# A fourth seven-product pair in each MLP layer, and an earlier release of the ring slots of summed blocks

## The chip, the cores and the metric

The kernel runs on one core of a Trainium2 chip. Its time is the device time of one execution in microseconds (us); less is better. The engines are named as in the profile: PE (matrix products), DVE (vector), ACT (scalar), POOL (the general one, which here issues small transfers) and SP (which issues the loads of the weights). They run at the same time, each through its own program in order, and wait for one another through semaphores.

## What is computed

A network of three blocks on 256 tokens of width 2048, all in float32. The change lies in the MLP of the first two blocks (depth 2, width 8192):

```python
def squared_relu_mlp(h, w1, w2):
    z = jax.nn.relu(h @ w1)
    return (z * z) @ w2
# h: 256 x 2048, w1: 2048 x 8192, w2: 8192 x 2048; once in each of two layers
x = x + squared_relu_mlp(rms_norm(x, ffn_norm[i]), w_ff1[i], w_ff2[i])
```

Before and behind the MLPs stand projections, attention, a recurrent unit and a third block, which the change leaves as they are.

## The kernel before

**Slabs.** Every weight is read once from DRAM in slabs of 256 rows by 512 columns (512 KB). A product of the 256 x 2048 activations with 512 columns of a weight is a group (`g14`, `g15`, ...) of eight slabs. A slab goes through four steps: SP loads it into one of four slots of the ring `raw`; ACT rounds it into `whi`; DVE subtracts and writes the rest into `wlo`; PE multiplies. `whi` and `wlo` have four slots too, so ACT can't begin slab n before PE is done with slab n-4 (`act.wait_ge(mm, n + 1 - RAW)`). The precision of float32 is kept by three products (activation high by `whi`, high by `wlo`, low by `whi`), for two rows of 128 in the slab and two halves of 128 tokens: 12 matmuls of 128x512.

**Seven products for eight.** For some pairs of groups of `w_ff1` the 2 x 2 blocks (two halves of the tokens, two halves of the 2048 rows, two groups of 512 columns) are multiplied in Winograd's form of Strassen's scheme: seven products instead of eight, with sums of blocks as factors. Such a pair has seven stages `p1`, `p2`, `p5`, `p3`, `p6`, `p7`, `p4` of four half slabs each. A half slab is a slab that is multiplied with one half of the tokens only: 6 matmuls. The pair is 28 half slabs (168 matmuls) in place of 16 slabs (192 matmuls), and each half slab is rounded and split like a slab. The sums are built in four buffers `chain_raw` (`qk`, `prob` and two halves of `mkv`): `p1` is loaded straight into them; for `p5`, `p6` and `p4` DVE adds a raw block to them (`chain_sum`), and ACT and DVE then split the sum, not the raw block; for `p7` DVE writes a difference into the raw slot (`u3`). DVE does these sums two tasks ahead: behind the split of task n stands the sum for task n+2. A pair loads 24 slabs (`p6` loads none, it sums the block of `p3` once more).

**The order.** `plan()` writes it out by hand. A slab has a number v, eight to a group; `number_all` puts a half slab behind the slab v at which `pair_of` has set it (28 half slabs spread evenly from `first` to `last`), and numbers all tasks n. Other work stands in lists for each engine under a v and runs when the engine has done its part of slab v: so `epi_add`, with which DVE adds a finished group of `w_ff2` from PSUM (`acc[g % 2]`) to x, and the parts of a pair's end (`part_n2`, `part_n1`, `relu_...`, `part_square`, `turned`: 16 small transfers issued by POOL, then `tail`). Group g uses the same half of PSUM as group g-2, so PE begins it only when the `epi_...` of group g-2 is done:

```python
if begins:
    if of >= 2:
        pe.wait_ge(out_of[of % 2], of // 2)
```

**The layers.** An MLP is cut into four chunks of 2048 columns of `w_ff1`, each followed by the four groups of `w_ff2` that use it. `PAIRS` says for each chunk how many of its two pairs of groups take the seven products. The half slabs of a chunk are woven into the slabs of the chunk ahead of it, since they depend on nothing of it. Below, f is the number v of the first `w_ff2` slab of the chunk they are woven into; in layer 0 the third chunk has f = 208. A layer takes 3 pairs in the kernel before, 2 layers 6 pairs.

Of the kernel before, what the change touches and what calls it, by code (L numbers as in the profile page):

```python
# [308 lines left out]
FF2_EVEN = ((0, 1), (2, 3), (4, 5), (6, 7))  # L309


PAIRS = (0, 1, 1, 1)


STAGES = (("p1",), ("p2",), ("p5",), ("p3", "p6"), ("p7",), ("p4",))
CHAIN = {"p1": 0, "p5": 1, "p6": 2, "p4": 3}
BLOCKS = {"p1": (0, 0), "p2": (1, 0), "p5": (0, 1), "p3": (1, 1), "p6": (1, 1), "p7": (0, 0), "p4": (1, 0)}
SUMS = {"p5": 0, "p7": 1, "p3": 2, "p6": 3}
QUARTERS = NK // 2 // SLAB_K


def plan():
# [92 lines left out]
    def ffn(layer, rst, a, z, next_rst, next_gain):  # L415

        waiting = []
        for c, count in enumerate(PAIRS):
            gs = [sc.group(f"w_ff1{layer}", 0, D * c + GW * i, a) for i in range(2 * count, 4)]
# [25 lines left out]
            for n, left in at_need:  # L445
                sc.groups[fs[n // S]].need[n % S] = [("tail_lo", sc.tails - left)]
            more = PAIRS[c + 1] if c < NCHUNK - 1 else 0
            if more == 1:
# [180 lines left out]
def build(nc, A, out):  # L629
# [6 lines left out]
    with ctx:  # L636
# [7 lines left out]
        def sem(name):  # L644
            return ctx.enter_context(nc.semaphore(name))
# [161 lines left out]
        sm = {n: sem(n) for n in names}  # L807
# [17 lines left out]
        def raw_of(task):  # L825
            return raw[:, task.raw * SLAB:(task.raw + 1) * SLAB]
# [5 lines left out]
        def tokens(t, lo, n, width):  # L832

            return t[:, 0:TB * width].rearrange("p (b n) -> p b n", b=TB)[:, :, lo:lo + n]
# [38 lines left out]
        def block_of(part, stage):  # L873

            k, n = BLOCKS[stage]
            pair = sc.pairs[part.pair]
            row, col = P * (k * NK // 2 + SLAB_K * part.j), D * pair.chunk + pair.col + GW * (1 - n)
            return W[f"w_ff1{pair.layer}"][row:row + SLAB_K * P, col:col + GW].rearrange("(t p) n -> p t n", p=P)

        def chained(part, stage):  # L880

            if stage == "p1":
                return sm[f"chain_in{part.j}"], 16 * (part.pair + 1)
            return sm["chain_add"], QUARTERS * (3 * part.pair + CHAIN[stage] - 1) + part.j + 1

        def in_rows(t):
            return t.rearrange("p (t n) -> p t n", t=SLAB_K)
# [41 lines left out]
        @block.sync  # L929
        def _(sp):  # L930
            def slot_free(task):

                last = task.before
                if last is None:
                    return
                if last.part and last.part.stage == "p3":
                    sp.wait_ge(sm["chain_add"], QUARTERS * (3 * last.part.pair + CHAIN["p6"] - 1) + last.part.j + 1)
                sp.wait_ge(w_lo, last.n + 1)

            def slab(task):  # L940
                of, k, _, _ = sc.slab_of(task.g, task.s)
                of = sc.groups[of]
                slot_free(task)
                dst = raw_of(task)
                row = of.row + k * SLAB_K * P
                src = W[of.w][row:row + SLAB_K * P, :]
                if of.pieces:
                    src = src[:, 0:2 * QKW].rearrange("(t p) (m c) -> p t m c", p=P, m=2)
                    dst = dst.rearrange("p (t m c) -> p t m c", t=SLAB_K, m=2)
                    for k in range(SLAB_K):  # L950
                        sp.dma_start(dst[:, k], src[:, k, :, of.col:of.col + GW // 2])\
                            .then_inc(ld[task.raw], 16)
                else:
                    sp.dma_start(in_rows(dst), src[:, of.col:of.col + GW].rearrange("(t p) n -> p t n", p=P))\
                        .then_inc(ld[task.raw], 16)

            def part_load(task):
                part = task.part
                if part.stage == "p6":
                    return  # L960
                if part.stage == "p1":
                    pair = sc.pairs[part.pair]
                    if pair.first:
                        sp.wait_ge(sm["sum_lo"], 4 * (pair.layer + 1))
                    else:
                        sp.wait_ge(w_lo, sc.pairs[part.pair - 1].parts["p4", part.j].n + 1)
                    sp.dma_start(in_rows(chain_raw[part.j]), block_of(part, "p1"))\
                        .then_inc(sm[f"chain_in{part.j}"], 16)
                    return
                slot_free(task)  # L970
                sp.dma_start(in_rows(raw_of(task)), block_of(part, part.stage))\
                    .then_inc(ld[task.raw], 16)

            def memory(i):

                sp.dma_start(tokens(mem, GW * i, GW, D),
                             A["mem"][0].rearrange("(b p) n -> p b n", p=P)[:, :, GW * i:GW * (i + 1)])\
                    .then_inc(sm[f"mem{i}_in"], 16)

            for task in sc.stream:  # L980
                if task.part:
                    part_load(task)
                    continue
                if task.n < D // GW:
                    memory(task.n)
                slab(task)

            o = out[0].rearrange("(b p) n -> p b n", p=P)
            for i, (b, c, n) in enumerate(FINAL):
                sp.wait_ge(sm["fin_ok"], i + 1)  # L990
                sp.dma_start(o[:, b, c:c + n], y[:, D * b + c:D * b + c + n]).then_inc(sm["out_done"], 16)
            sp.wait_ge(sm["out_done"], 16 * len(FINAL))
# [125 lines left out]
        def _(act):  # L1118
# [9 lines left out]
            def hi(task, fold=None):  # L1128
                part, n = task.part, task.n
                c = slice(task.slot * SLAB, (task.slot + 1) * SLAB)  # L1130
                if part and part.stage in CHAIN:
                    act.wait_ge(*chained(part, part.stage))
                    src = chain_raw[part.j]
                else:
                    src = raw_of(task)
                    if part and part.stage == "p7":
                        act.wait_ge(sm["u3_ok"], QUARTERS * part.pair + part.j + 1)
                    else:
                        act.wait_ge(ld[task.raw], 16 * task.loads)
                if n >= RAW:  # L1140
                    act.wait_ge(mm, n + 1 - RAW)
                if fold is None:
                    A_(whi[:, c], src, ACT.Copy).then_inc(w_hi, 1)  # L1143
                    return
                for (t, c), (_, r) in zip(rows_of(task.slot), rows_of(task.raw)):
                    ins = A_(whi[:, c], raw[:, r], ACT.Copy, scale=gain_of(fold, SLAB_K * task.s + t))  # L1146
                ins.then_inc(w_hi, 1)
# [347 lines left out]
        def _(dve):  # L1495
# [22 lines left out]
            def u3(task):  # L1518

                dve.wait_ge(ld[task.raw], 16 * task.loads)  # L1520
                dve.wait_ge(*chained(task.part, "p6"))
                V.tensor_tensor(raw_of(task), chain_raw[task.part.j], raw_of(task), ALU.subtract).then_inc(sm["u3_ok"], 1)

            def chain_sum(task):

                part = task.part
                if part.stage == "p6":
                    task = sc.stream[sc.pairs[part.pair].parts["p3", part.j].n]
                t = chain_raw[part.j]
                dve.wait_ge(ld[task.raw], 16 * task.loads)  # L1530
                dve.wait_ge(*(chained(part, "p1")))
                V.tensor_tensor(t, t, raw_of(task), ALU.add).then_inc(sm["chain_add"], 1)  # L1532
# [941 lines left out]
```

## Time and profile before

| | us |
|---|---|
| median of 3 runs (2952.87 to 2954.57) | 2954.24 |
| the profiled execution's own time | 2953.56 |
| its span, first to last instruction | 2951.8 |
| PE busy | 2914.2 |
| DVE busy | 2054.6 |
| ACT busy | 1619.7 |

The span is what the trace shows; 1.8 us of the profiled execution's own time lie around it. Matmuls overlap in their records (each is shown with 390 ns, the next starts 227 ns later), so a busy PE is not a measure of its speed; what counts is whether PE waits, and the distance from one matmul's start to the next. The sums of the pairs (L1532) run from 370.3 to 807.6 us in the first MLP, and the last one of the second starts at 1892.9 us.

### The profile page before, as it was taken

The numbers are of one execution on the slowest core, as the hardware profiler recorded it, in microseconds if no ns is written. First come the engines' busy times: TensorE is split into PE (matmuls) and PEld (weight loads), VectorE is DVE, ScalarE is ACT, GpSimd is POOL, SyncE is SP. The second block draws the span as 40 slices with busy tenths as digits, with TensorE's granted clock in tenths as the row PEclk, the third lists the DMA queues.
The fourth block names the chain that finished last, engine by engine and source line by source line (L and its number), as shares of the span: only waits on it lengthen the run. The fifth ranks groups of instructions, "written<-read, shape, count | busy, mean of one in ns | idle before, by whom it ended". The sixth has DMA issues, their size and how long they took to land.

```text
span 2951.8 us, 35199 instructions
## 1 busy us (share of the span) xinstructions
PE 2914.2 (99%) x12996; PEld 2399.3 (81%) x12996; DVE 2054.6 (70%) x2679; ACT 1619.7 (55%) x2134; POOL 634.6 (21%) x1257
## 2 busy tenths in 40 slices
PE   8999999999999999999999999999999999999998
PEld 7888888888888778788888888888888887878887
DVE  6537777777766777877786777856557777887555
ACT  6445555555554566755655555545444456775433
POOL 0003312212033310013212122123324663100210
PEclk9999999999999999999999999999999999999999
DMA  7446777776677655556767777766776776666774
GB/s 264 165 151 202 237 231 248 230 253 221 227 228 234 206 171 161 166 167 213 242 222 247 228 248 236 233 215 217 236 216 199 220 227 187 209 205 207 249 255 157
DMA packets 351628, 636.94 MB, mean 216 GB/s; under 512 B 38240, under 2 KB 63200, under 8 KB 350688
## 3 DMA queue, kind: packets, MB, share of 16 engines
q1 hardware_dynamic: 306448, 566.30, 60.6%
q0 software_dynamic: 44432, 67.45, 7.2%
q8 instruction: 102, 1.67, 0.2%
q10 hardware_dynamic: 576, 0.94, 0.1%
q14 instruction: 70, 0.57, 0.1%
HBM read 586.31 MB, written 10.49 MB: 202 GB/s over the span
## 4 chain that ended last, share of the span: by engine, by line
PE 85%; DVE 8%; ACT 3%; DMA 2%; issue 1%; DVEq 0%; ACTq 0%
PE acc L2153 25%; PE acc L2155 25%; PE acc L2154 25%; DVE wlo L1516 2%; DMA raw<-in_w_ff 2%; PE tp L2191 1%; PE tp L2192 1%; PE tp L2193 1%; PE sd L2193 1%; PE sd L2191 1%; PE sd L2192 1%; DVE wlo L1509 1%; ACT whi L1143 1%; PE tp L2360 1%; PE sd L2254 0%
## 5 line engine op out<-in xcount | busy, mean ns | idle before, releaser
L1516 DVE TENSOR_TENSOR wlo<-raw,whi 128x1024 fp32r<-128x1024 f32 x920 | 1112.5, 1220 | 570.9 <-ACT whi L1143 565.0
L2153 PE MATMUL acc<-whi,set_hi 128*128 128x512 f32 x3696 | 1458.5, 395 | 15.9 <-DVE wlo L1516 10.4
L2155 PE MATMUL acc<-whi,set_lo 128*128 128x512 f32 x3696 | 1439.9, 390 | 0.0
L2154 PE MATMUL acc<-wlo,set_hi 128*128 128x512 f32 x3696 | 1439.4, 389 | 0.0
L1143 ACT ACTIVATE whi<-raw 128x1024 fp32r<-128x1024 f32 x920 | 960.5, 1057 | 711.5 <-PE acc L2155 478.7
L2153 PEld LDWEIGHTS acc<-whi,set_hi 128*128 128x128 f32 x3696 | 694.5, 188 | 177.1 <-DVE wlo L1516 19.3
L2155 PEld LDWEIGHTS acc<-whi,set_lo 128*128 128x128 f32 x3696 | 694.2, 188 | 145.8
L2154 PEld LDWEIGHTS acc<-wlo,set_hi 128*128 128x128 f32 x3696 | 694.7, 188 | 143.4 <-issue 1.9
L1106 POOL DMA_DIRECT2D u<-u x832 | 406.9, 498 | 1440.2 <-DVE u L1708 1334.5
L1509 DVE SCALAR_TENSOR_TENSOR wlo<-raw,par,whi 128x512 fp32r<-128x512 f32 x160 | 111.6, 746 | 47.1 <-ACT whi L1146 46.4
L1146 ACT ACTIVATE whi<-raw,par 128x512 fp32r<-128x512 f32 x160 | 104.2, 715 | 22.9 <-PE acc L2155 11.1
L1106 POOL DMA_DIRECT2D kv<-kv x112 | 55.0, 499 | 173.2 <-DVE kv L1708 169.1
L1143 ACT ACTIVATE whi<-mkv 128x1024 fp32r<-128x1024 f32 x48 | 51.0, 1062 | 71.7 <-DVE mkv L1532 43.1
L1615 DVE TENSOR_TENSOR x<-acc,x 128x1024 f32<-128x1024 f32 x40 | 48.8, 1220 | 26.2 <-PE acc L2155 26.2
L1516 DVE TENSOR_TENSOR wlo<-mkv,whi 128x1024 fp32r<-128x1024 f32 x48 | 58.4, 1217 | 12.1 <-ACT whi L1143 11.3
L1532 DVE TENSOR_TENSOR mkv<-mkv,raw 128x1024 f32<-128x1024 f32 x36 | 44.0, 1221 | 26.2 <-DMA raw<-in_w_ff 26.1
L1690 DVE TENSOR_TENSOR set_lo<-u,set_hi 128x1024 fp32r<-128x1024 f32 x44 | 53.6, 1219 | 12.1 <-ACT set_hi L1323 12.0
L1143 ACT ACTIVATE whi<-prob 128x1024 fp32r<-128x1024 f32 x24 | 25.5, 1062 | 49.5 <-DVE prob L1532 32.4
L1708 DVE STREAM_TRANSPOSE u<-stage_b 128x512 f32<-128x512 f32 x80 | 51.9, 687 | 0.0
L1106 POOL DMA_DIRECT2D x<-kv x64 | 36.8, 584 | 59.0 <-DVE kv L1720 54.5
L1143 ACT ACTIVATE whi<-qk 128x1024 fp32r<-128x1024 f32 x24 | 25.5, 1063 | 41.7 <-DVE qk L1532 31.8
L1285 ACT ACTIVATE qk<-x 128x512 f32<-128x512 f32 x40 | 25.0, 629 | 40.6 <-DVE x L1615 40.6
(346 smaller groups left out, 2201.5 us busy)
## 6 DMA issues: line engine op xcount, KB each, us to landing
raw<-in_w_ff SPq DMA_DIRECT2D x536, 512.0 KB, 4.6
raw<-in_w_in SPq DMA_DIRECT2D x248, 512.0 KB, 4.5
raw<-in_w_out SPq DMA_DIRECT2D x96, 512.0 KB, 4.6
u<-u POOLq DMA_DIRECT2D x832, 32.0 KB, 3.8
raw<-in_w_mem_kv SPq DMA_DIRECT2D x32, 512.0 KB, 4.5
raw<-in_w_proj_a SPq DMA_DIRECT2D x32, 512.0 KB, 4.7
raw<-in_w_proj_b SPq DMA_DIRECT2D x32, 512.0 KB, 7.4
raw<-in_w_kv SPq DMA_DIRECT2D x48, 256.0 KB, 3.4
```

The source lines that it names most:

```text
L1106: dma(to, of).then_inc(sm["shuffled"], 16)
L1143: A_(whi[:, c], src, ACT.Copy).then_inc(w_hi, 1)
L1146: ins = A_(whi[:, c], raw[:, r], ACT.Copy, scale=gain_of(fold, SLAB_K * task.s + t))
L1509: ins = V.scalar_tensor_tensor(out=wlo[:, c], in0=raw[:, r], scalar=gain_of(fold, SLAB_K * task.s + t), in1=whi[:, c].bitcast(f32), op0=AL ...
L1516: V.tensor_tensor(wlo[:, c], src, whi[:, c].bitcast(f32), ALU.subtract).then_inc(w_lo, 1)
L1690: ins = V.tensor_tensor(in_blocks(l[:, c]), tp, in_blocks(h[:, c]).bitcast(f32), ALU.subtract)
L2153: T.matmul(o, h[:, tok], whi[:, c], start=first, stop=False)
L2154: T.matmul(o, h[:, tok], wlo[:, c], start=False, stop=False)
L2155: ins = T.matmul(o, l[:, tok], whi[:, c], start=False, stop=last)
L2191: T.matmul(o, h, whi[:, c], start=first, stop=False, skip_group_check=True)
L2192: T.matmul(o, h, wlo[:, c], start=False, stop=False, skip_group_check=True)
L2193: ins = T.matmul(o, l, whi[:, c], start=False, stop=last, skip_group_check=True)
```

## The change

It does two things. The last entry of `PAIRS` goes from 1 to 2: both pairs of groups of the fourth chunk are now done in seven products (8 pairs in all). And the load that reuses the ring slot of a `p5` or `p4` block waits for that block's sum (`chain_add`), no longer for its split (`w_lo`).

```diff
-PAIRS = (0, 1, 1, 1)
+PAIRS = (0, 1, 1, 2)
...
+        def summed(part, stage):
+            return sm["chain_add"], QUARTERS * (3 * part.pair + CHAIN[stage] - 1) + part.j + 1
+
         def chained(part, stage):
 
             if stage == "p1":
                 return sm[f"chain_in{part.j}"], 16 * (part.pair + 1)
-            return sm["chain_add"], QUARTERS * (3 * part.pair + CHAIN[stage] - 1) + part.j + 1
+            return summed(part, stage)
...
                 last = task.before
                 if last is None:
                     return
-                if last.part and last.part.stage == "p3":
-                    sp.wait_ge(sm["chain_add"], QUARTERS * (3 * last.part.pair + CHAIN["p6"] - 1) + last.part.j + 1)
+                stage = last.part.stage if last.part else None
+                if stage in ("p5", "p4"):
+                    sp.wait_ge(*summed(last.part, stage))
+                    return
+                if stage == "p3":
+                    sp.wait_ge(*summed(last.part, "p6"))
                 sp.wait_ge(w_lo, last.n + 1)
```

With 2 in `PAIRS`, code of `ffn` runs that the kernel before has but never reaches (`more` is the entry of the next chunk):

```python
elif more == 2:
    sc.weave(fs[2], fs[3], FF2_EVEN)      # ((0, 1), (2, 3), (4, 5), (6, 7)): two slabs of each group in turn
    first, middle = (f - 21, f + 6) if c else (f - 11, f + 9)
    p = seven(layer, c + 1, a, 0, first, middle - 1)
    q = seven(layer, c + 1, a, 2 * GW, middle, f + 29)
    drain(p, "n2", rst, z, 0, f + 12, f + 23)
    drain(p, "n1", rst, z, 4, f + 24, f + 29)
    drain(q, "n2", rst, z, 8, f + 31, f + 37)
    drain(q, "n1", rst, z, 12, f + 38, f + 44)
for i, g in enumerate(fs):
    e = sc.end(g)
    if c < NCHUNK - 1:
        sc.at("dve", e + (1 if i == 0 else 2 if more == 2 and i > 1 else 3), "epi_add", g, GW * i)
```

So in the third chunk of each layer the one pair that stood at v = 194 to 234 (28 half slabs on 40 slabs) becomes two pairs at v = 187 to 213 and 214 to 237 (56 half slabs on 50 slabs), and the 16 slabs of `w_ff1` in the fourth chunk (v = 240 to 255, with no half slab between them) are gone. Line numbers behind the first edit in `build` are 7 higher in the changed kernel.

**Place 1: where group g29 (the fourth `w_ff2` group of the third chunk) begins.** DVE before, at the `epi_add` of g27 (`x<-acc,x`, L1615), which stands under v = 227; g29 begins at v = 232, five slabs later:

```order
434 L1516 TENSOR_TENSOR wlo<-raw,whi 128x1024 x3
435 L1522 TENSOR_TENSOR raw<-mkv,raw 128x1024
436 L1615 TENSOR_TENSOR x<-acc,x 128x2x512
437 L1516 TENSOR_TENSOR wlo<-raw,whi 128x1024 x2
438 L1532 TENSOR_TENSOR qk<-qk,raw 128x1024
439 L1516 TENSOR_TENSOR wlo<-raw,whi 128x1024
```

DVE in the changed kernel: row 474 is the split of g29's first slab (v = 226, task 325), row 475 that of a `p6` half slab (task 326), row 476 that of the slab v = 227 (task 327), and row 477 the same `epi_add` of g27:

```order
472 L1523 TENSOR_TENSOR wlo<-raw,whi 128x1024
473 L1539 TENSOR_TENSOR prob<-prob,raw 128x1024
474 L1523 TENSOR_TENSOR wlo<-raw,whi 128x1024
475 L1523 TENSOR_TENSOR wlo<-prob,whi 128x1024
476 L1523 TENSOR_TENSOR wlo<-raw,whi 128x1024
477 L1622 TENSOR_TENSOR x<-acc,x 128x2x512
478 L1523 TENSOR_TENSOR wlo<-raw,whi 128x1024
```

PE in the changed kernel at the same place: a `p3` half slab (task 324, `tp<-...`, 6 matmuls) and then the first matmul of g29 (task 325), which waits for that `epi_add` (`group_out1`):

```order
3353 L2198 MATMUL tp<-whi,sum_hi 128x512 [waits w_lo]
3354 L2199 MATMUL tp<-wlo,sum_hi 128x512
3355 L2200 MATMUL tp<-whi,sum_lo 128x512
3356 L2198 MATMUL tp<-whi,sum_hi 128x512
3357 L2199 MATMUL tp<-wlo,sum_hi 128x512
3358 L2200 MATMUL tp<-whi,sum_lo 128x512
3359 L2160 MATMUL acc<-whi,set_hi 128x512 [waits group_out1,w_lo]
```

The wait of g29's first slab thus moves from five slabs behind its `epi_add` to one slab ahead of it.

**Place 2: the queue of SP in the second chunk.** L971 (before) and L978 (changed) load half slabs, L954 and L961 slabs of `w_ff2`. Before, around the stages `p5` and `p3` of the second pair:

```order
82 L971 DMA raw<-in_w_ff 128x2x512 [waits w_lo]
83 L954 DMA raw<-in_w_ff 128x2x512 [waits w_lo] x2
84 L971 DMA raw<-in_w_ff 128x2x512 [waits w_lo]
85 L954 DMA raw<-in_w_ff 128x2x512 [waits w_lo]
86 L971 DMA raw<-in_w_ff 128x2x512 [waits w_lo]
87 L954 DMA raw<-in_w_ff 128x2x512 [waits w_lo] x3
88 L971 DMA raw<-in_w_ff 128x2x512 [waits w_lo,chain_add]
```

The same loads in the changed kernel:

```order
89 L978 DMA raw<-in_w_ff 128x2x512 [waits w_lo]
90 L961 DMA raw<-in_w_ff 128x2x512 [waits w_lo]
91 L961 DMA raw<-in_w_ff 128x2x512 [waits chain_add]
92 L978 DMA raw<-in_w_ff 128x2x512 [waits w_lo]
93 L961 DMA raw<-in_w_ff 128x2x512 [waits chain_add]
94 L978 DMA raw<-in_w_ff 128x2x512 [waits w_lo]
95 L961 DMA raw<-in_w_ff 128x2x512 [waits w_lo]
96 L961 DMA raw<-in_w_ff 128x2x512 [waits chain_add]
97 L961 DMA raw<-in_w_ff 128x2x512 [waits w_lo]
98 L978 DMA raw<-in_w_ff 128x2x512 [waits w_lo,chain_add]
```

The loads and their order are the same; the ones that reuse a `p5` slot wait for the sum alone.

## Rows read from the trace of the kernel before

**Rows 1.** The page: busy time of each engine.
```profile
span 2951.8 us, 35199 instructions
...
PE 2914.2 (99%) x12996; PEld 2399.3 (81%) x12996; DVE 2054.6 (70%) x2679; ACT 1619.7 (55%) x2134; POOL 634.6 (21%) x1257
```
**Rows 2.** PE's waits, 320 to 870 us (total, times, longest).
```profile
PE acc L2153 <- DVE wlo L1516: 1.2, 2, 0.6
```
**Rows 3.** PE's waits, 1390 to 1960 us.
```profile
PE acc L2153 <- DVE wlo L1516: 0.5, 2, 0.3
```
**Rows 4.** Timeline of PE: first matmuls of a slab, a half slab, a slab.
```profile
425.70 0.39 PE L2153 MATMUL acc<-whi,set_hi 128*128 128x512 f32 x1
...
428.42 0.39 PE L2191 MATMUL sd<-whi,sum_hi 128*128 128x512 f32 x1
...
429.78 0.39 PE L2153 MATMUL acc<-whi,set_hi 128*128 128x512 f32 x1
```
**Rows 5.** Timeline of ACT, 408 to 416 us (start, duration, idle time before).
```profile
409.63 1.06 ACT L1143 ACTIVATE whi<-raw 128x1024 fp32r<-128x1024 f32 x1 [1.66 <-PE acc L2155]
411.00 1.06 ACT L1143 ACTIVATE whi<-raw 128x1024 fp32r<-128x1024 f32 x1 [0.30 <-PE sd L2193]
413.71 1.06 ACT L1143 ACTIVATE whi<-raw 128x1024 fp32r<-128x1024 f32 x1 [1.66 <-PE acc L2155]
```
**Rows 6.** Busy time by stretch: the first, the second and the third pair.
```profile
core 0: us, PE busy (x) PEld busy (x) DVE busy (x) ACT busy (x) POOL busy (x), PEclk, DMA share, GB/s
320.00:475.00 155.00, 154.43 (x682) 127.59 (x681) 118.77 (x108) 88.67 (x91) 25.69 (x53) 1.00 0.73 234
475.00:640.00 165.00, 164.36 (x725) 135.51 (x724) 119.90 (x108) 90.44 (x92) 29.03 (x60) 1.00 0.73 236
```
**Rows 7.** DVE's groups, 320 to 870 us (count, busy us, mean ns, idle before, releaser).
```profile
L1516 DVE TENSOR_TENSOR wlo<-raw,whi 128x1024 fp32r<-128x1024 f32 x197 | 239.8, 1221 | 104.0 <-ACT whi L1143 102.0
...
L1532 DVE TENSOR_TENSOR mkv<-mkv,raw 128x1024 f32<-128x1024 f32 x18 | 22.0, 1221 | 11.2 <-DMA raw<-in_w_ff 11.2
L1708 DVE STREAM_TRANSPOSE u<-stage_b 128x512 f32<-128x512 f32 x28 | 18.2, 687 | 0.0
L1690 DVE TENSOR_TENSOR set_lo<-u,set_hi 128x1024 fp32r<-128x1024 f32 x14 | 17.0, 1218 | 0.0
...
L1615 DVE TENSOR_TENSOR x<-acc,x 128x1024 f32<-128x1024 f32 x12 | 14.6, 1217 | 0.0
...
L1573 DVE TENSOR_TENSOR ob<-tp,ob 128x512 f32<-128x512 f32 x2 | 1.4, 684 | 0.0
```
**Rows 8.** All sums (L1532) and differences (L1522): idle time of DVE before them.
```profile
L1532 DVE TENSOR_TENSOR mkv<-mkv,raw x36: 1216/1219/1228, 380.6 to 1892.9; 128x1024 f32<-128x1024 f32 x36
...
  DMA raw<-in_w_ff: 55.2, 32
...
  DMA raw<-in_w_ff: 12.9, 18
```
**Rows 9.** Timeline of DVE in stage p5 of the second pair.
```profile
535.82 1.23 DVE L1516 TENSOR_TENSOR wlo<-qk,whi 128x1024 fp32r<-128x1024 f32 x1
537.21 1.23 DVE L1516 TENSOR_TENSOR wlo<-raw,whi 128x1024 fp32r<-128x1024 f32 x1 [0.16 <-ACT whi L1143]
542.40 1.22 DVE L1532 TENSOR_TENSOR prob<-prob,raw 128x1024 f32<-128x1024 f32 x1 [3.96 <-DMA raw<-in_w_ff]
543.54 1.22 DVE L1516 TENSOR_TENSOR wlo<-raw,whi 128x1024 fp32r<-128x1024 f32 x1
```
**Rows 10.** Timeline of SP there: when that load was issued.
```profile
535.85 0.37 SPq L971 DMA_DIRECT2D raw<-in_w_ff  x1
```
**Rows 11.** Loads of L954 (160), 320 to 870 us: from issue to landing.
```profile
DMA to landing us min/median/max: 3.4/4.7/7.3
```

## The prediction

> **What bounds the kernel now.** The page comes first: PE is busy 99% of the span, DVE 70%, ACT 55% [rows 1]. Since matmul records overlap, that alone doesn't show PE as the bound, so I read PE's own waits over the stretches of the pairs: 1.2 us in 550 us of the first MLP and 0.5 us in 570 us of the second [rows 2, 3]. There PE is hardly ever starved, and what it has to do is the time. The timeline gives its price: a slab of 12 matmuls takes 428.42 - 425.70 = 2.72 us, a half slab of 6 takes 429.78 - 428.42 = 1.36 us, so one matmul 0.227 us [rows 4]. ACT shows the same from the other side: it waits for PE before nearly every rounding, since `whi` has only four slots, and begins when PE ends a task [rows 5]. The other engines have room on average: DVE is busy 118.8 of 155 us (77%) on the first pair, 119.9 of 165 us (73%) on the second, and the loads bring 234 to 236 GB/s [rows 6]. The room isn't even, though. DVE works in order and a sum waits for its own load: 55.2 us before the 72 sums (36 into `mkv`, as many into `qk` and `prob`) and 12.9 us before the 24 differences, 0.71 us each over all 96 [rows 8]. The worst I found stands in stage p5 of the second pair: DVE idle 3.96 us until 542.40, for a load that SP issued at 535.85 [rows 9, 10]. PE didn't suffer much because the split runs ahead of it. In the rhythm of [rows 5] ACT begins task n when PE ends n-4, and the split is done 1.06 + 1.23 us later, about 2.3 [rows 5, 9]; PE needs it after tasks n-3 to n-1, 5.4 or 6.8 us with slabs and half slabs in turn. That lead of 3.1 to 4.5 us is what absorbs a late load.
>
> **What the change takes from PE.** In each layer one more pair of groups of `w_ff1` is 168 matmuls in place of 192. 2 layers x 24 x 0.227 us = **10.9 us less**, all on the bound. Its last loads, splits and sums move into the third chunk.
>
> **What it adds to the feed.** Per layer 12 more roundings and splits, 8 more loads, 16 sums or differences. They don't cost by themselves; the question is whether DVE and the loads still keep ahead where all now lies. The third chunk's stretch from the first half slab (v = 187) to the last (v = 237) has 50 slabs and 56 half slabs: PE 50 x 2.72 + 56 x 1.36 = 212 us. DVE has 106 splits and 32 sums. One behind the other they start 1.13 us apart (542.40, 543.54 [rows 9]): 157 us. Its other work there: 6 tails, 5 turns of 2 x 0.65, 4 `epi_add`, 10 operations of 128x512, at the durations of [rows 7] less the overlap about 6.8 + 6.5 + 4.5 + 6 = 24 us. That is 181 of 212 us, 85%. With the mean wait of 0.71 us before 32 sums it is 204 us, 96%. The second pair in the kernel before, counted alike, is 40 slabs and 28 half slabs, 147 us of PE against some 115 + 11 = 126 us, 86%, and lost next to nothing. So the feed goes from 86% to 96% of PE's pace: still below it, but the lead will be used up wherever a wait, a tail and a turn fall together. The places are stage p5 and stages p7/p4 of each of the two pairs, where every half slab brings a sum: four a layer. Lower bound of the loss: nothing, as PE lost nothing there so far [rows 2]. Upper bound: a wait as in [rows 9], 4 us, at three of the four places beyond what the lead takes, at 2 us each, 6 us a layer. The demand is nearer to the pace than before but not over it, so I take 0.5 us a place, 2 us a layer: **+4.0 us**.
>
> **The new wait at g29.** Place 1 of the change shows it. PE may begin task 325, g29's first slab, only behind the `epi_add` of g27, which DVE has behind the split of task 327. ACT can't round 327 before PE ends 323. From there: rounding 1.06 us, split 1.23, `epi_add` 1.13 behind it, hand-overs 0.1 to 0.2, so 3.6 us; PE has only task 324, 1.36 us, to do meanwhile [rows 5, 7, 9]. PE stands still for 2.2 us in each layer even when all else is in time; queued behind it are all further matmuls, and nothing hides it. **+4.4 us**, 8 if DVE comes late from stage p5 just ahead by 2 us. After it the lead is whole again. The other waits of this kind have room by the same count: `epi_add` of g28 stands at the first slab of the fourth chunk, whose group needs it, and is done about 3 us before PE comes; the last tail (v = 252, needed at v = 252) has 4.6 us; the first pair's `part_n2` and `part_n1` stand 5 or more tasks ahead of who waits for them.
>
> **The earlier release.** SP issues in order. The load that reuses a p5 or p4 slot now goes out when the split of the task before is done, one task earlier: 1.1 to 2.7 us. It moves none of the loads of p5's first two half slabs, those of p7, nor the one of [rows 9, 10]. On the six old pairs there is little to win, as PE waits 1.7 us in all [rows 2, 3]; I take **-0.5 us**, bounds 0 and -2. In the dense stretch its help is already in my 2 us a layer.
>
> **A rule beside it.** The trace has 3.4 us from issue to landing at the shortest, 4.7 at the median, 7.3 at the longest [rows 11]. The Trainium skill, DMA: Bandwidth & Descriptors, section "Anatomy of one DMA", puts a transfer at 2 us fixed and its bytes at 436 GB/s, by which a slab would take an estimated 3.2 us. By that no sum would wait for a load, and the dense stretch would cost nothing. It agrees with the shortest only; other loads in flight are in the median, so I go by the rows.
>
> **The sum.** Against the profiled execution's own time: 2953.6 - 10.9 + 4.0 + 4.4 - 0.5 = 2950.6 us. The median of the runs is 0.7 us above that execution: **2951.2 us**. What a measurement here can tell from no change is about 0.2%, 5.9 us, so the likeliest case is "no difference", 3.0 us faster. Its own range: 2 us a layer may be 1 or 3.5, so 2949 to 2955.
>
> **Rivals.**
> 1. *The feed keeps ahead.* The lead absorbs all of it, as it does now, and the dense stretch costs nothing: -10.9 + 4.4 - 0.5 to -2 = -7 to -8.5, 2946.5 us. For it: 85% without waits, and [rows 2]. Against: 96% with them. 24%.
> 2. *DVE takes over as the bound.* Place: the 50 slabs of the third chunk. Price: (181 + 32 w - 212 - the lead of 4) us a layer, w the mean wait before a sum. At w = 0.71 it is below nothing; at w = 1.2 the layer loses 3.4 us, which with 2.2 us at g29 is the whole gain of 5.4: from there on the change makes the kernel slower. At w = 1.3 it is 6.6 us a layer, -10.9 + 13.2 + 4.4 - 0.5 = +6.2, 2960.5 us; at 1.4, 10 us a layer and 2 more in all at g29, +15, 2969 us. For it: the loads are denser, 98 slabs of 0.524 MB in 212 us are 242 GB/s with the small transfers on top, and a load in company takes longer [rows 11]; the longest waits are 4 us. Against: when DVE is late, its loads have landed and w shrinks; the earlier release takes a task's time off two of four loads in p5 and p4. 17%.
> 3. *The change doesn't bring its matmuls' worth.* Were the four last groups bound by something else, 48 matmuls fewer would give nothing; with PE's waits at 1.7 of 1120 us I leave it 1%.
>
> **Chances and range.** Forecast within 0.2%: 58%. Rival 1 ends on both sides of the bound of 2948.3; with the forecast's lower tail, faster is 26%. Slower by over 0.2% (above 2960.1) is most of rival 2, 15%; the same is 59%. For 8 in 10 the range reaches to the bottom of rival 1 and into rival 2: 2945.5 to 2961.
>
> **What would show it.** 48 matmuls fewer and still 0.227 us each. A wait of PE for `x<-acc,x` of about 2.2 us, once a layer, near v = 226. PE's other waits for the split `wlo` in the two third chunks: 2 us a layer if I am right, none by rival 1, over 6 by rival 2, with DVE's mean wait for loads at its sums near 0.7, under it, or over 1.2 us. The fourth chunks should run without waits. I am wrong if PE's new waits stand somewhere else, above all in ACT's work (a tail, two relus and a square in one place) or at a transfer of POOL.

## The result, and the profile after

The changed kernel takes 2961.9 us (median of 14 runs, 2957.6 to 2966.5), the kernel before 2954.5 us in the same comparison (14 runs, 2951.9 to 2956.9). The ratio is 1.0026, 95% interval 1.0020 to 1.0033: slower by 7.5 us, where 2951.2 was forecast and 2961 was the upper end of the range. The profiled execution took 2962.0 us. In some of the comparisons below one execution took 1.2 to 4.9 times as long as the rest; the ratios leave it out.

The page of the changed kernel shows that PE did get less to do (48 matmuls fewer, 12948 against 12996 in [rows 1]), in a longer span:

```profile
span 2960.2 us, 35299 instructions
...
PE 2910.9 (98%) x12948; PEld 2390.5 (81%) x12948; DVE 2122.2 (72%) x2745; ACT 1643.5 (56%) x2164; POOL 634.3 (21%) x1257
```

The views that answer to [rows 2, 3] are PE's waits around the two third chunks of the changed kernel, 600 to 880 us and 1690 to 1960 us (total, times, longest):

```profile
PE acc L2160 <- DVE wlo L1523: 4.5, 6, 1.4
PE acc L2160 <- DVE x L1622: 2.3, 1, 2.3
PE tp L2198 <- DVE wlo L1523: 0.2, 1, 0.2
...
PE acc L2160 <- DVE x L1622: 2.3, 1, 2.3
PE acc L2160 <- DVE wlo L1523: 2.0, 3, 0.9
PE tp L2198 <- DVE wlo L1523: 0.4, 1, 0.4
```

The `x` row is g29's first matmul behind the `epi_add` of g27, as forecast: once a layer, 2.3 us. The `wlo` rows are the feed, 4.7 and 2.4 us. Together the waits are 11.7 us and don't yet explain the result (10.9 us of matmuls saved, and still 8.4 us more in the span). The timeline of PE shows what they leave out (start, duration, idle time in brackets):

```profile
796.35 0.50 PE L2160 MATMUL acc<-whi,set_hi 128*128 128x512 f32 x1 [1.38 <-DVE wlo L1523]
...
815.24 0.39 PE L2200 MATMUL tp<-whi,sum_lo 128*128 128x512 f32 x1
817.96 0.75 PE L2160 MATMUL acc<-whi,set_hi 128*128 128x512 f32 x1 [2.34 <-DVE x L1622]
818.51 0.63 PE L2161 MATMUL acc<-wlo,set_hi 128*128 128x512 f32 x1
818.94 0.63 PE L2162 MATMUL acc<-whi,set_lo 128*128 128x512 f32 x1
...
821.46 0.40 PE L2162 MATMUL acc<-whi,set_lo 128*128 128x512 f32 x1
821.70 0.39 PE L2160 MATMUL acc<-whi,set_hi 128*128 128x512 f32 x1
```

Behind the wait of 2.34 us the next matmuls start 0.43 us apart (818.51, 818.94), and only from 821.46 on 0.24 and 0.23 us. The clock says why. These are the stretches of the changed kernel around that place, with PEclk as the last figure but two:

```profile
660.00:850.00 190.00, 184.54 (x801) 150.86 (x800) 157.34 (x143) 111.33 (x115) 32.36 (x67) 0.99 0.74 236
...
800.00:810.00 10.00, 9.04 (x40) 7.13 (x39) 9.66 (x9) 6.14 (x6) 0.00 (x0) 1.00 0.73 242
810.00:815.00 5.00, 5.00 (x23) 4.13 (x22) 4.40 (x4) 3.24 (x4) 0.00 (x0) 1.00 0.65 222
815.00:820.00 5.00, 2.66 (x8) 1.87 (x7) 4.87 (x5) 1.48 (x2) 0.00 (x0) 0.80 0.67 228
820.00:825.00 5.00, 5.00 (x20) 4.05 (x20) 1.31 (x2) 2.06 (x2) 0.00 (x0) 0.86 0.32 105
...
1905.00:1910.00 5.00, 3.76 (x10) 3.03 (x11) 3.36 (x3) 0.06 (x1) 0.00 (x0) 0.68 0.50 147
```

From 815 to 820 and from 820 to 825 us the mean granted clock is 0.80 and 0.86, in the second layer 0.68 between 1905 and 1910. The records behind these means hold one stretch of 3.41 us at 0.5 at each of the two places (the lower level, 1.2 GHz) and 1.0 on both sides of it. PE had stood idle for 2.3 us. The Trainium skill, "TensorE: Matmul & The Clock Gate", Part 1, gives 426.7 ns from start to start for 512 columns at that level, and the rows agree: 818.94 - 818.51 = 0.43.

To have every loss in one unit I took the distance from the end of each task to the end of the next and subtracted 2.72 us for a slab and 1.36 us for a half slab [rows 4]. The sums by place:

| loss in us | before | changed, layer 0 | changed, layer 1 |
|---|---|---|---|
| pairs of the first two chunks | 3.2 in both layers | 1.5 | 0.4 |
| third chunk, v = 211 to 213 | 0 | 1.4 | 1.8 |
| v = 222, 223 (`p5` of the second pair) | 0 | 3.0 | 1.4 |
| v = 226 (g29 begins) | 0 | 4.2 | 4.2 |
| v = 234 to 237 (`p4` of the second pair) | 0 | 2.4 | 1.1 |
| third chunk in all | 0 | 11.1 | 8.6 |

The last line also has some small ones. So the third chunks lose 19.7 us. With the 10.9 us saved and 1.3 us less lost in the old pairs that is +7.5 us, and the spans differ by 8.4. g29's 4.2 us are 815.24 to 817.96 less one matmul, 2.5 us of standing still, and 1.7 us for the eight matmuls behind it, 0.2 us each.

The other large item is stage `p5`. Timeline of DVE in the changed kernel, first there and then ahead of g29:

```profile
793.93 1.23 DVE L1539 TENSOR_TENSOR mkv<-mkv,raw 128x1024 f32<-128x1024 f32 x1 [2.79 <-DMA raw<-in_w_ff]
...
799.27 1.23 DVE L1539 TENSOR_TENSOR mkv<-mkv,raw 128x1024 f32<-128x1024 f32 x1 [1.25 <-DMA raw<-in_w_ff]
...
815.45 1.23 DVE L1523 TENSOR_TENSOR wlo<-raw,whi 128x1024 fp32r<-128x1024 f32 x1
816.60 1.22 DVE L1622 TENSOR_TENSOR x<-acc,x 128x1024 f32<-128x1024 f32 x1
```

the roundings of ACT that waited there for loads of their own:

```profile
792.67 1.06 ACT L1150 ACTIVATE whi<-raw 128x1024 fp32r<-128x1024 f32 x1 [2.79 <-DMA raw<-in_w_ff]
...
797.68 1.06 ACT L1150 ACTIVATE whi<-raw 128x1024 fp32r<-128x1024 f32 x1 [1.44 <-DMA raw<-in_w_ff]
```

and the issues of SP and of POOL at the same time:

```profile
785.35 0.37 SPq L961 DMA_DIRECT2D raw<-in_w_ff  x1
785.76 0.47 SPq L978 DMA_DIRECT2D raw<-in_w_ff  x1
789.94 0.37 SPq L961 DMA_DIRECT2D raw<-in_w_ff  x1
790.36 0.48 SPq L978 DMA_DIRECT2D raw<-in_w_ff  x1
...
787.09 7.81 POOL L1113 DMA_DIRECT2D u<-u  x16 [28.13 <-DVE u L1715]
```

The two half slabs whose sums wait were issued at 785.76 and 790.36 and are there at 793.9 and 799.3: 8.2 and 8.9 us, longer than any load of [rows 11]. The two slabs loaded beside them (785.35 and 789.94) took 7.3 and 7.7 us until ACT could round them, so all four loads were late, not only those of the sums. POOL issued its 16 small transfers in just that time. The whole trace shows the same: of 174 loads of `w_ff1` and `w_ff2` issued during such a burst (from 2 us before its first transfer to its last) 61 took over 6.5 us, with a median of 5.6 us; of 357 issued clear of one (over 4 us before its first transfer or over 2 us behind its last), 20 did, with a median of 4.4 us. After it DVE works 9.66 of 10 us (800 to 810) to catch up. The mean wait at the sums has not grown; the same view as [rows 8] for the changed kernel:

```profile
  DMA raw<-in_w_ff: 55.5, 37
```

That is 55.5 us before 96 sums, 0.58 us each, against 55.2 before 72.

### The profile page after: what moved, and what is told of

It is laid out like the page before. It is cut to its first block, busy times and chain, and to the rows that moved or that the text cites. A ratio compares the mean times of both kernels' runs of the same rounds, so it can differ in the third digit from the quotient of the medians.

```text
span 2960.2 us, 35299 instructions
## 1 busy us (share of the span) xinstructions
PE 2910.9 (98%) x12948; PEld 2390.5 (81%) x12948; DVE 2122.2 (72%) x2745; ACT 1643.5 (56%) x2164; POOL 634.3 (21%) x1257
## 4 chain that ended last, share of the span: by engine, by line
PE 80%; DVE 11%; ACT 4%; DMA 3%; issue 2%; DVEq 0%; ACTq 0%; SPq 0%
PE acc L2160 23%; PE acc L2162 22%; PE acc L2161 22%; DVE wlo L1523 3%; DMA raw<-in_w_ff 2%; PE tp L2198 1%; PE tp L2200 1%; PE tp L2199 1%; PE sd L2198 1%; PE sd L2200 1%; PE sd L2199 1%; ACT whi L1150 1%; DVE wlo L1516 1%; DVE ob L1967 1%; PE tp L2367 1%
## 5 line engine op out<-in xcount | busy, mean ns | idle before, releaser
L2160 PE MATMUL acc<-whi,set_hi 128*128 128x512 f32 x3568 | 1411.8, 396 | 26.9 <-DVE wlo L1523 16.8
L2162 PE MATMUL acc<-whi,set_lo 128*128 128x512 f32 x3568 | 1390.9, 390 | 0.0
L2161 PE MATMUL acc<-wlo,set_hi 128*128 128x512 f32 x3568 | 1390.5, 390 | 0.0
L2160 PEld LDWEIGHTS acc<-whi,set_hi 128*128 128x128 f32 x3568 | 670.9, 188 | 189.7 <-DVE wlo L1523 32.7
L2162 PEld LDWEIGHTS acc<-whi,set_lo 128*128 128x128 f32 x3568 | 670.7, 188 | 141.7
L2161 PEld LDWEIGHTS acc<-wlo,set_hi 128*128 128x128 f32 x3568 | 671.4, 188 | 137.5 <-issue 1.9
L1153 ACT ACTIVATE whi<-raw,par 128x512 fp32r<-128x512 f32 x160 | 104.3, 715 | 22.2 <-PE acc L2162 10.9
L1150 ACT ACTIVATE whi<-mkv 128x1024 fp32r<-128x1024 f32 x64 | 67.9, 1061 | 84.4 <-DVE mkv L1539 59.1
L1523 DVE TENSOR_TENSOR wlo<-mkv,whi 128x1024 fp32r<-128x1024 f32 x64 | 78.0, 1219 | 16.0 <-ACT whi L1150 14.8
L2198 PE MATMUL sd<-whi,sum_hi 128*128 128x512 f32 x128 | 49.8, 389 | 0.0
L2200 PE MATMUL sd<-whi,sum_lo 128*128 128x512 f32 x128 | 49.8, 389 | 0.0
```

The source lines that it names most:

```text
L1523: V.tensor_tensor(wlo[:, c], src, whi[:, c].bitcast(f32), ALU.subtract).then_inc(w_lo, 1)
L2160: T.matmul(o, h[:, tok], whi[:, c], start=first, stop=False)
L2161: T.matmul(o, h[:, tok], wlo[:, c], start=False, stop=False)
L2162: ins = T.matmul(o, l[:, tok], whi[:, c], start=False, stop=last)
L2198: T.matmul(o, h, whi[:, c], start=first, stop=False, skip_group_check=True)
L2200: ins = T.matmul(o, l, whi[:, c], start=False, stop=last, skip_group_check=True)
```

## The experiments

Each one is compared with the kernel before on its own chip; to set runs of different chips beside each other I use the ratios, 0.001 being 2.95 us.

**The wait at g29 taken away.** In the changed kernel the `epi_add` of g27 goes from v = 227 to v = 225:

```diff
-sc.at("dve", e + (1 if i == 0 else 2 if more == 2 and i > 1 else 3), "epi_add", g, GW * i)
+sc.at("dve", e + (1 if i == 0 or more == 2 and i == 1 else 2 if more == 2 and i > 1 else 3), "epi_add", g, GW * i)
```

> The changed kernel with the addition of g27 to x put two slabs earlier on DVE (behind the split of v = 225 instead of v = 227), nothing else. My theory: at g29 PE waits 2.3 us for this addition in each layer and then does its next 8 matmuls at half the clock, 0.427 us apart instead of 0.227 (1.0 and 0.5 granted), about 2 us more; with the wait gone both go, 2 x 4.2 = 8.4 us faster than the changed kernel: about 2953.5 us. Rival (the wait is what costs, the low clock stands there by chance and would come elsewhere): 4.4 us, about 2957.5. Rival (DVE is late there anyhow, and PE would wait for the split wlo instead): no difference, 2962.

Measured: 2951.5 us, ratio 0.9996 (0.9988 to 1.0005), some 9 us less than the changed kernel. PE's waits, 600 to 880 us:

```profile
PE acc L2160 <- DVE wlo L1523: 3.9, 6, 2.0
PE tp L2198 <- DVE wlo L1523: 0.4, 1, 0.4
PE acc L2160 <- DVE x L1622: 0.3, 1, 0.3
```

The wait for `x` is 0.3 us and nowhere in the MLPs is the granted clock under 1.0. The third chunks lose 11.3 us in place of 19.7, that is 8.4 less, what g29 had cost; the feed's losses stay. The kernel is now equal to the one before: the 10.9 us saved are eaten by the feed. Where the feed loses changes, though its sum stays: stage `p5` of layer 0 loses 0.1 us here in place of 3.0, `p4` 3.7 in place of 2.4. The longest wait left is this one, and the clock stays at 1.0 behind it:

```profile
858.26 0.50 PE L2160 MATMUL acc<-whi,set_hi 128*128 128x512 f32 x1 [2.00 <-DVE wlo L1523]
```

The variants from "The small transfers made small" on start from this one; those between start from the changed kernel or the kernel before, as said at each.

**The two halves of the change apart.** First both pairs with the old rule of release (`slot_free` without the branch for `p5` and `p4`):

```diff
-                if stage in ("p5", "p4"):
-                    sp.wait_ge(*summed(last.part, stage))
-                    return
```

> The changed kernel with the old release of the ring slots: a p5 or p4 slot is given free by its split, all four pairs stay. If the earlier release carries the dense third chunk, as I assumed, the losses there rise from 5.6 us a layer besides g29 to 8 or more, and the six old pairs give back 1.3 us: 5 to 8 us slower than the changed kernel, about 2968 us. Rival (the loads are late for another reason than the slot, since SP issues in order): within 2 us of 2962.

Then the new release with the old `PAIRS = (0, 1, 1, 1)`:

> The kernel before with the earlier release alone (PAIRS as before). By PE's time from task to task in the two traces the old pairs lost 3.2 us before and 1.8 us with the new release: so about 1.5 us faster than before, 2953 us, and within 0.2% in any case. Rival (loads that go out earlier only wait beside each other): no difference, 2954.5.

Measured: 2960.4 us, 1.0024 (1.0016 to 1.0033), and 2953.0 us, 0.9998 (0.9989 to 1.0006). So the release makes no difference that can be measured, with three pairs or with four. My theory for the old release (some 2968 us, since the earlier one carries the dense third chunk) was wrong, and the rival was right. The trace of this run has more to tell. At g29 PE waits the same 2.3 us in both layers. In layer 0 the clock falls for 3.4 us; in layer 1 it doesn't, as its row of PE's timeline and the stretches around it show:

```profile
1904.04 0.47 PE L2157 MATMUL acc<-whi,set_hi 128*128 128x512 f32 x1 [2.34 <-DVE x L1619]
```

```profile
1900.00:1905.00 5.00, 2.66 (x12) 1.94 (x11) 4.69 (x5) 2.26 (x3) 0.00 (x0) 1.00 0.74 243
1905.00:1910.00 5.00, 5.00 (x23) 4.11 (x23) 2.79 (x4) 2.12 (x2) 0.00 (x0) 1.00 0.48 167
```

g29 loses 4.19 us in the first and 2.62 in the second: the same wait with and without the lower clock, which makes 1.6 us of difference.

**The wait alone, in the kernel before.** There the `epi_add` of g27 is moved from v = 227 to v = 233, one slab behind g29's begin, with three pairs a layer:

```diff
-sc.at("dve", e + (1 if i == 0 else 2 if more == 2 and i > 1 else 3), "epi_add", g, GW * i)
+sc.at("dve", e + (1 if i == 0 else 9 if c == 2 and i == 1 else 3), "epi_add", g, GW * i)
```

> The disputed cost by itself: the kernel before (6 pairs, old release) with the addition of g27 put at v = 233, one slab behind the begin of g29 at v = 232, in each third chunk. PE's tasks around it are the same as in the changed kernel (a slab, a half slab, a slab), so PE waits 2.2 to 2.3 us there, twice. If only the wait counts: 4.5 us slower than before, 2958 us. If the engine comes back at half its clock after such a wait (1.0 to 0.5 granted for some 3.4 us): up to 4.2 us each, 8.4 us slower, 2962 us; with the low clock in one of the two, 6.5 us slower.

Measured: 2968.4 us, 1.0048 (1.0035 to 1.0062), 14.7 us more than the kernel before beside it, also more than the 2962 us expected. PE's waits, 640 to 880 us and 1600 to 2000 us, the stretches around the first of them, and DVE just ahead of its end:

```profile
PE acc L2153 <- DVE x L1615: 5.4, 1, 5.4
...
PE acc L2153 <- DVE x L1615: 4.4, 1, 4.4
```

```profile
805.00:810.00 5.00, 0.87 (x2) 0.81 (x3) 3.38 (x3) 2.24 (x3) 0.00 (x0) 0.82 0.61 226
810.00:815.00 5.00, 5.00 (x13) 3.89 (x13) 1.33 (x3) 0.32 (x1) 3.13 (x7) 0.50 0.44 136
```

```profile
806.62 1.22 DVE L1532 TENSOR_TENSOR mkv<-mkv,raw 128x1024 f32<-128x1024 f32 x1 [1.86 <-DMA raw<-in_w_ff]
807.76 1.22 DVE L1615 TENSOR_TENSOR x<-acc,x 128x1024 f32<-128x1024 f32 x1
```

The wait came out longer than meant, since here, other than in the changed kernel, a sum stands between the split and the `epi_add`: it takes 1.14 us itself (806.62 to 807.76) and waits for its load, 1.86 us in the first layer and 0.56 in the second. Counted as in the changed kernel, PE stands still for 5.6 and 4.6 us, and the matmuls behind lose another 2.7 us each time, while the clock is at 0.5 for 6.8 us. So the mechanism stands without any fourth pair, and both waits of over 4 us had a longer stretch at the lower clock behind them than those of 2.3 us.

**The small transfers made small.** POOL's 16 transfers for each finished group of `staged` move rows of 64 B in place of 1 KB, as many as before:

```diff
...
+                        if t in staged_tails:
+                            to, of = to[:, 0:16], of[:, 0:16]
                         dma(to, of).then_inc(sm["shuffled"], 16)
```

> As the run with the early addition, and the small transfers that turn the MLP's staged results (16 per turn, issued by POOL) move 64 bytes a row instead of 1 KB; their number, order and waits stay. It leaves out most of that data, so the MLP's second factor is incomplete. If these transfers are what makes the loads of p5 and p4 take 7 to 9 us in the third chunk, the loss there besides g29 (11 us in two layers) falls by half or more: 5 to 9 us faster than the run with the early addition. Rival (the loads of the weights hold each other up): within 2 us of it.

Measured: 2947.6 us, 0.9981 (0.9971 to 0.9990), 4.4 us less than with the `epi_add` early alone, a little under the 5 to 9 us expected. The third chunks lose 6.3 us, not 11.3; of 576 loads of the MLPs' weights 40 take over 6.5 us, where it was 70. Of those issued during a burst of POOL 25 do, where it was 47. PE's waits, 600 to 880 us:

```profile
PE acc L2165 <- DVE wlo L1528: 1.1, 3, 0.6
```

So the bytes of these transfers, half a megabyte each time, hold up the loads beside them. The Trainium skill, "DMA: Bandwidth & Descriptors", section "Queues, rings and completion order", says that a DMA engine takes turns between the queues that have work, packet by packet; that fits, though no run here shows the turns themselves.

**The loads made short.** Of each half slab's load behind `p1` only 128 of the 512 columns are brought:

```diff
-sp.dma_start(in_rows(raw_of(task)), block_of(part, part.stage))\
+sp.dma_start(in_rows(raw_of(task))[:, :, 0:GW // 4], block_of(part, part.stage)[:, :, 0:GW // 4])\
```

> As the run with the early addition (2951.5 us), but the loads of all half slabs behind stage p1 bring 128 of 512 columns (128 KB in place of 512 KB); the rest of the slot keeps old data, so the output is not the reference's. Splits, sums and products stay. It splits what is left of the loss in the two third chunks (11.3 us there besides nothing at g29): stalls from late loads go, stalls from the engines' own work stay. My theory after the run with small moves: the stalls in p4 of the second pair (v = 235 to 237) go, those behind the cluster at v = 211 to 213 (a tail, two relus, a square, a turn and part_n2; 2.1 us a layer) stay: loss of 4 to 5 us, 2945 us. Rival (loads cause all): loss near 0, 2940 us. Rival (DVE's work causes all): 2951 us.

Measured: 2942.9 us, 0.9962 (0.9949 to 0.9976), 10.0 us less than with the `epi_add` early alone, near the 2945 us of my theory; the rival that DVE's work causes all (2951 us) falls. The sums' wait for loads is nearly gone:

```profile
  DMA raw<-in_w_ff: 7.1, 8
```

Every loss of the third chunks is gone with it but one, the same in both layers to a hundredth: 0.46 us at the `p4` half slab of v = 212 and 0.90 us at the slab v = 213, 2.7 us in all. So of the 11.3 us 8.6 go with the loads' bytes and 2.7 come from work that stands in one place. This variant takes traffic away altogether, so it doesn't tell how much of the 8.6 us each half slab's own load costs and how much what stands beside it. ACT there, and DVE:

```profile
740.11 1.04 ACT L1324 ACTIVATE set_hi<-u 128x1024 fp32r<-128x1024 f32 x1
741.05 1.25 ACT L1253 ACTIVATE stage_a<-acc,small 128x512 f32<-128x512 f32 x2
742.33 1.06 ACT L1211 ACTIVATE stage_b<-stage_a 128x1024 f32<-128x1024 f32 x1
743.29 1.04 ACT L1150 ACTIVATE whi<-prob 128x1024 fp32r<-128x1024 f32 x1
...
744.37 1.23 DVE L1523 TENSOR_TENSOR wlo<-prob,whi 128x1024 fp32r<-128x1024 f32 x1 [1.78 <-ACT whi L1150]
...
747.78 1.30 DVE L1715 STREAM_TRANSPOSE u<-stage_b 128x512 f32<-128x512 f32 x2
749.00 0.65 DVE L1592 TENSOR_TENSOR stage_a<-sd,scan 128x512 f32<-128x512 f32 x1
749.58 0.68 DVE L1593 TENSOR_TENSOR stage_a<-tp,scan 128x512 f32<-128x512 f32 x1
750.18 1.21 DVE L1523 TENSOR_TENSOR wlo<-mkv,whi 128x1024 fp32r<-128x1024 f32 x1
```

A tail, two relus and a square keep ACT from the next rounding for 3.2 us (740.11 to 743.29); DVE waits 1.78 us for it and then has a turn and `part_n2` (2.4 us) ahead of the split that PE wants.

**Four tries to move the work instead.** Turns and tails of the third chunk set apart (`drain(p, ...)` with `f + 9, f + 21` and `f + 22, f + 27`, the tail of g25 three slabs earlier):

> The early addition, and the two turns of the first pair's results in the third chunk put where no sums are: at v = 217 (stage p2 of the second pair) and v = 230 in place of 220 (p5) and 232 (p7 and p4), with the tails they need moved along (216, 229, 235). If the small transfers hold up the loads of the stages with sums, the stalls at v = 222, 223 and 235 to 237 shrink (5.5 us in the run before it): 2 to 4 us faster than that run, 2948.5 us. Rival (transfers hold up any load, and the stage doesn't matter, since v = 230 still reaches into p7): no difference, 2951.5.

The same with the tail of g24 at v = 209:

> As the run with the turns moved, and the tail of g24's result two slabs earlier (v = 209), apart from the relus and square of v = 211. If that cluster on ACT and DVE makes the stall at v = 212 and 213 (2 us a layer), moving one of its four operations takes away 1 us a layer at least: 2 to 3 us faster than the run with the turns moved, 2946 us. Rival (the stall is from DVE's sums and waits for loads, and ACT has time): no difference.

`part_n2` of the first pair one slab later:

```diff
-        sc.at("dve", add, "part_" + of, p)
+        sc.at("dve", add + (1 if (p, of) in ((2, "n2"), (6, "n2")) else 0), "part_" + of, p)
```

> The changed kernel with epi_add of g27 under v = 225 and one more move: part_n2 of the third chunk's first pair stands on DVE under v = 213 (layer 1: 533) instead of 212, so it no longer stands ahead of the splits of the last two tasks of v = 212. Theory (the stall of 1.4 us a layer that short loads did not take away comes from work that stands close together on DVE: turn 1.3 us, part_n2 1.2 us): 1.2 us less ahead of these splits, the stall at v = 212 and 213 falls by 1 us a layer or more, about 2951.0 against 2953.2 without the move. Rival (the rounding of p4.1, late behind the tail, two relus and a square on ACT, sets the stall; or part_n2 only delays the tasks of v = 213 and p1.0 of the next pair, whose first product waits for it): the same loss, at v = 213 or 214, and no difference.

And the second pair spread over two slabs more (`middle, f + 31`):

> The changed kernel with epi_add of g27 under v = 225 and the third chunk's second pair spread to f + 31 instead of f + 29, so 28 half slabs stand on 26 slabs, not on 24. Theory (the half slabs stand too close together for the loads: stalls where p5 and p4 of the second pair wait for their loads, about 8 us in both layers): fewer loads in the same time, half of the loss at v = 222 to 237 goes, 3 to 4 us less, about 2949.5. Rival (the loads are late because of the small transfers and of a queue of four slots, at each bunch of transfers, however the half slabs are spread): the stalls move by a slab or two and stay, 2953.

Measured:

| | us | ratio (interval) | loss in the third chunks |
|---|---|---|---|
| `epi_add` early alone | 2951.5 | 0.9996 (0.9988 to 1.0005) | 11.3 |
| turns moved | 2955.7 | 1.0004 (0.9995 to 1.0014) | 11.1 |
| and the tail | 2954.9 | 1.0005 (0.9996 to 1.0014) | 12.0 |
| `part_n2` later | 2953.3 | 0.9994 (0.9985 to 1.0003) | 10.2 |
| wider spread | 2966.6 | 1.0047 (1.0033 to 1.0060) | 8.7, and 15.3 at v = 246, 247 |

None of the three variants below the first line, up to `part_n2` later, differs from it by what can be told, so the gains of 2 to 4 us expected of the moved turns and of the tail didn't come. That bears on the small transfers too: moving a burst out of the stages with sums helped nothing, only making it small did. With the turns moved v = 222 and 223 lose nothing in layer 0, but a new stall of 1.8 us stands at v = 540 in layer 1; with the tail apart the stall at v = 212 stays at 1.3 and 1.6 us. With `part_n2` later that stall falls from 2.3 to 0.3 us in layer 1 and stays at 2.0 in layer 0, while `p5` and `p4` of layer 1 lose 1.5 us more: the stall went in one layer of two, and the time didn't change.

The wider spread answers its own question: v = 222 to 239 lose 4.2 us in both layers together in place of 5.7. That is a quarter, not the half expected, and the kernel is slower by 15 us, not faster by 4. What I hadn't seen is that `drain` puts the turn two slabs later with the pair, while the tail that uses its transfers stays at v = 245. Its rows of PE, ACT and POOL:

```profile
891.31 0.80 PE L2160 MATMUL acc<-whi,set_hi 128*128 128x512 f32 x1 [4.72 <-DVE wlo L1523]
...
885.68 1.06 ACT L1324 ACTIVATE set_hi<-u 128x1024 fp32r<-128x1024 f32 x1 [8.81 <-DMA u<-u]
...
873.07 7.84 POOL L1113 DMA_DIRECT2D u<-u  x16 [25.59 <-DVE u L1715]
```

POOL needs 7.84 us to issue the 16 transfers, they have landed 12.6 us after the first issue, ACT stands still for 8.81 us (3.06 us at the same place with the pair two slabs shorter), and PE loses 7.5 us at v = 246, with the clock at 0.5 for 6.8 us once more, in each layer.

## Why the prediction was wrong

- **The matmuls, -10.9: right.** 48 fewer at 0.227 us each. With loads cut short the kernel is 11.2 us faster than the one before (7 to 15 by its interval). That variant is also rid of the 3.2 us that the old pairs lost, and it keeps 2.7 in the third chunks, by which 10.9 + 3.2 - 2.7 = 11.4 would be expected: PE's work was the bound, and the gain was there to be had.
- **g29, +4.4: right place and mechanism, size wrong.** The wait is 2.3 us in each layer (2.2 forecast), but costs 4.2. The step that failed: I priced a wait of PE at its own length, as if the engine came back at full pace. It came back at a granted clock of 0.5 for 3.4 us, 1.7 us more each time, and some 0.2 us pass at the restart. This term measured 8.4 us; removing the wait gave back 9. The "8" that I named as its upper case was for another reason, a late DVE, and that is not what happened.
- **The feed of the third chunk, +4.0: too small.** It measured 11.3 us, 6.9 in layer 0 and 4.4 in layer 1. The failing step is "0.5 us a place": I took the average (85% of PE's pace, 96% with the mean wait) and [rows 2] as signs that the lead absorbs nearly all. DVE's share was about as worked out (157.3 of 190 us, 83%), and the mean wait even fell, to 0.58 us at the sums. But late loads stand together: in stage `p5` of layer 0 two sums waited 2.79 and 1.25 us one behind the other, where I had given the lead 3.1 to 4.5 us and each sum has a split behind it. That the two waits together are what used the lead up is my reading of this one stage; no run varied the lead. My upper bound of 6 us a layer held for the mean, 5.6, and not for layer 0. Of the 11.3 us 8.6 went when the loads were cut short, and 4.4 to 5.0 when only the small transfers were, which I had only in the line on what could prove me wrong; the other 2.7 us stand at v = 212 and 213, behind the tail, relus, square, turn and `part_n2`.
- **The release, -0.5: not distinguishable from nothing.** The old pairs lost 1.3 us less in the one profile, but alone it gave 0.9998 (0.9989 to 1.0006).
- **Rival 2, DVE as the bound,** gave nearly the right time for a wrong reason: its condition was a mean wait above 1.2 us. Rival 1 falls, rival 3 too. The rule by which a load takes 3.2 us, and the dense stretch nothing, falls with rival 1. The Trainium skill, "DMA: Bandwidth & Descriptors", section "Anatomy of one DMA", has the 2 us and the 436 GB/s for transfers that GpSimd issues. These slabs are loaded by SP, which the prediction passed over; no run here measures such a load by itself.
- **The sum.** g29 4.0 us over, the feed 7.3 over, the old pairs 0.8 under: 10.5 of the 11.4 us by which the profiled execution exceeds the 2950.6 of my sum. The last 0.9 us lie outside the MLPs, most of it behind 2622 us of the changed kernel, and stay unexplained.

Still open: what decides whether the clock falls behind a wait of 2.3 us; it fell at three of four such places. What makes the loads late that are not beside small transfers is open too. A ring `raw` of five slots (4 KB more a partition), the direct test of the lead, wasn't tried. No variant that computes the whole network is measurably faster than the kernel before.

## What to carry to other kernels

Price a wait of the matrix engine by its length plus what its clock takes afterwards: here 1.7 us behind a wait of 2.3, 2.7 behind 4.4 and 5.4, and nothing behind those of up to 2.0. Several short waits were cheaper here than one of 2.3 us, so look first for the handover that lets the engine stand still in one piece.

When an engine's feed comes near its pace (here DVE was busy 83% of the third chunk), don't spread the loss evenly from the mean wait. Take the longest chain in one stage: the worst two transfers one behind the other, with everything that shares the transfer engines at that time, against the lead. And when an item of a hand-written order moves, follow all that is tied to it, and all that isn't: the turn moved and its tail did not.

## What the runs showed of the hardware that I hadn't expected

- A wait of 2.3 us was followed by 3.4 us at a granted clock of 0.5 at three of four places; waits of 4.4, 4.7, 4.8 and 5.4 us by 6.8 us of it each time. Once it was at 1.0, waits of up to 2.0 us (row 858.26) left it there in all twelve traces.
- 16 transfers of 32 KB (rows of 1 KB), issued by POOL over 7.8 us, stand beside loads of 512 KB that take 8.2 and 8.9 us in place of 4.7 at the median; in the changed kernel 61 of 174 loads issued during such a burst took over 6.5 us, 20 of 357 clear of one. The same number of transfers with rows of 64 B took some 5 us of PE's losses away.
